# The layer norms of a ten-norm transformer stack: first moments of the last quarter taken earlier, last turned half evicted by ScalarE and VectorE together

## The reference, cut to what matters

```python
def layer_norm(h, g, b):
    mu = jnp.mean(hf, axis=-1, keepdims=True)
    var = jnp.mean(jnp.square(hf - mu), axis=-1, keepdims=True)
    y = (hf - mu) * lax.rsqrt(var + LN_EPS) * g + b
...
h = layer_norm(DEEPNORM_ALPHA * h + mix, ln1_g[l], ln1_b[l])
h = layer_norm(DEEPNORM_ALPHA * h + ffn, ln2_g[l], ln2_b[l])
```

## Time and profile before

| what | value |
|---|---|
| median of 3 runs | 3101.78 us (3094.33 to 3101.92) |
| the profiled execution's own time | 3095.23 us |
| its span, first to last instruction | 3093.4 us |
| TensorE busy | 2988.8 us, 97% |
| VectorE busy | 1920.4 us, 62% |
| ScalarE busy | 1347.9 us, 44% |
| GpSimd busy | 132.4 us, 4% |
| mean granted TensorE clock | 0.989 |

### The profile page before, as it was taken

The page is one execution under the profiler, slowest core; times in us unless marked ns, Lnnn a source line. Parts: engine busy times, 40 slices in busy tenths (PEclk is TensorE's granted clock), DMA queues, the critical chain, the costliest instruction groups (busy, mean ns, idle before and its releaser), DMA issues. The chain is left out here.

```text
span 3093.4 us, 53809 instructions
## 1 busy us (share of the span) xinstructions
PE 2988.8 (97%) x20906; PEld 2608.6 (84%) x20906; DVE 1920.4 (62%) x3659; ACT 1347.9 (44%) x2053; POOL 132.4 (4%) x62
## 2 busy tenths in 40 slices
PE   8998999999999999999999999999998999999898
PEld 7697889899898869888989989887777979777797
DVE  4489864787647648986478764755534564543546
ACT  4442444444444544244444444445424444442444
POOL 0061000000000006100000000000000000000000
PEclk9999999999999999999999999999999999999999
DMA  5243354544555424335454455553234545223444
GB/s 214 93 180 123 123 191 177 193 154 155 190 183 197 164 97 171 128 135 191 178 192 147 163 190 194 186 191 123 96 136 150 189 178 214 73 96 136 156 185 150
DMA packets 68022, 493.59 MB, mean 160 GB/s; under 512 B 7576, under 2 KB 7584, under 8 KB 8352
## 3 DMA queue, kind: packets, MB, share of 16 engines
q1 hardware_dynamic: 67568, 490.42, 43.6%
q0 software_dynamic: 304, 1.06, 0.1%
HBM read 490.39 MB, written 1.06 MB: 159 GB/s over the span
## 5 line engine op out<-in xcount | busy, mean ns | idle before, releaser
L780 DVE TENSOR_TENSOR ring_l<-ring,tile_h 128x1024 fp32r<-128x1024 f32 x648 | 765.0, 1222 | 667.9 <-ACT tile_h L735 663.8
L735 ACT ACTIVATE tile_h<-ring 128x1024 fp32r<-128x1024 f32 x644 | 645.7, 1051 | 533.2 <-PE ps L666 445.3
L634 PE MATMUL ps<-x_h,tile_h 128*128 128x256 f32 x2016 | 575.5, 285 | 2.1 <-issue 2.1
L635 PE MATMUL ps<-x_l,tile_h 128*128 128x256 f32 x2016 | 570.0, 283 | 0.0
L636 PE MATMUL ps<-x_h,ring_l 128*128 128x256 f32 x2016 | 569.9, 283 | 0.0
L634 PEld LDWEIGHTS ps<-x_h,tile_h 128*128 128x128 f32 x2016 | 386.4, 192 | 3.1 <-issue 2.8
L635 PEld LDWEIGHTS ps<-x_l,tile_h 128*128 128x128 f32 x2016 | 386.5, 192 | 0.2
L636 PEld LDWEIGHTS ps<-x_h,ring_l 128*128 128x128 f32 x2016 | 386.3, 192 | 0.0
L739 ACT ACTIVATE arena<-ps 128x512 f32 (+1 forms) x160 | 95.6, 597 | 432.2 <-PE ps L636 346.5
L664 PE MATMUL ps<-tile_h,w_even 128*128 128x512 f32 x640 | 249.5, 390 | 3.6 <-DVE w_even L805 3.6
L664 PE MATMUL ps<-tile_h,w_odd 128*128 128x512 f32 x640 | 249.3, 390 | 0.6 <-DVE w_odd L805 0.6
(11 more groups left out here) (322 smaller groups left out, 5598.8 us busy)
## 6 DMA issues: line engine op xcount, KB each, us to landing
ring<-stream SPq DMA_DIRECT2D x464, 1024.0 KB, 4.8
cs<-consts SPq DMA_DIRECT2D x1, 1712.5 KB, 8.6
x<-x_in SPq DMA_DIRECT2D x1, 1024.0 KB, 5.1
arena<-scratch POOLq DMA_DIRECT2D x1, 1024.0 KB, 7.8
out<-x SPq DMA_DIRECT2D x2, 512.0 KB, 2.7
tab<-table SPq DMA_DIRECT2D x1, 1.0 KB, 8.4
scratch<-arena POOLq DMA_DIRECT2D x1, 12.0 KB, 5.0
```

What stands on the lines that cost most here:

```text
L634: nc.tensor.matmul(out, uh[:, c, f], x_h[:, c, :], start=(c == 0), stop=False)
L635: nc.tensor.matmul(out, uh[:, c, f], x_l[:, c, :], start=False, stop=False)
L735: nc.scalar.activation(tile_h[:, j % 2, n], slot(k + j)[:, n], ACT.Copy).then_inc(hi_ready, 1)
L780: nc.vector.tensor_tensor(low_of(k + j)[:, n], slot(k + j)[:, n], tile_h[:, j % 2, n].bitcast(F32), ALU.subtract).then_inc(lo_ready, 1)
```

## The change

Two things are changed in each norm. First, VectorE takes the `bn_stats` of quarter (1,0) right after it has normalised tile 0, ahead of the wait for the last quarter; before, it was taken after the residual of the last quarter. Second, the eight turned chunks of token tile 1 are divided: ScalarE evicts chunks 0 to 3 (bank 6), and VectorE chunks 4 to 7 (bank 7), with its own semaphore `xt_dve`, between the last normalised half and the multiply by gamma. VectorE waits there until all transposes of the norm are done. All waits for the whole of `xT` now ask for both engines' counts (`turned`), and those of single chunks for the one that makes them (`chunk_turned`).

```diff
+        def turned(eng, m):
+            eng.wait_ge(xt_ready, 2 * KC + (KC + KC // 2) * m)
+            if m:
+                eng.wait_ge(xt_dve, KC // 2 * m)
...
+        def chunk_turned(eng, m, c):
+            if m == 0:
+                eng.wait_ge(xt_ready, KC + c + 1)
+            elif c < KC // 2:
+                eng.wait_ge(xt_ready, 2 * KC + (KC + KC // 2) * (m - 1) + (KC + c + 1))
+            else:
+                eng.wait_ge(xt_dve, KC // 2 * (m - 2) + (c + 1))
...
                     if fb == 0:
-                        pe.wait_ge(xt_ready, 2 * KC * m + (KC + c + 1))
+                        chunk_turned(pe, m, c)
...
             act_turned(act, n + 1, 0, 6, KC, which)
-            act_turned(act, n + 1, 1, 0, KC, which)
+            act_turned(act, n + 1, 1, 0, KC // 2, which)
...
             def moments(tt):
-                nc.vector.bn_stats(st[:, tt, 0, :], halves(tt, 0))
+                if tt == 0:
+                    nc.vector.bn_stats(st[:, tt, 0, :], halves(tt, 0))
                 step.after(nc.vector.bn_stats(st[:, tt, 1, :], halves(tt, 1)))
...
             residual(1, 0)
             normalize(0)
+            nc.vector.bn_stats(st[:, 1, 0, :], halves(1, 0))
             finished(dve, block, l, added)
             step.after(residual(1, 1))
             moments(1)
             normalize(1)
+            dve.wait_ge(xt_mm, 4 * n + 8)
+            for c in range(KC // 2, KC):
+                nc.vector.tensor_scalar(xT[:, c, P:2 * P], ps[7][:, (c - KC // 2) * P:(c - KC // 2 + 1) * P],
+                                        gb[:, which, 0, c:c + 1], gb[:, which, 1, c:c + 1],
+                                        ALU.mult, ALU.add).then_inc(xt_dve, 1)
             arrived(dve, block, l, k)
...
-            act.wait_ge(xt_ready, 4 * KC * l + 2 * KC)
+            turned(act, 2 * l)
             act_split_x(act)
...
-                pool.wait_ge(xt_ready, 6 * KC * l + (4 * LAYERS + 2) * KC)
+                turned(pool, 2 * LAYERS + 3 * l)
```

More of the change, by code:

```diff
@@ L211, in program @@
         acc_first, ln_half = sem("acc_first"), sem("ln_half")
-        xt_mm, xt_ready = sem("xt_mm"), sem("xt_ready")
+        xt_mm, xt_ready, xt_dve = sem("xt_mm"), sem("xt_ready"), sem("xt_dve")
         dve_step = sem("dve_step")
@@ L352, in carry_wait, with dve_norm @@
             nc.vector.memset(spare[:, cell:cell + 1], 0.0)
-        def dve_norm(dve, step, n, block, l, k, added):
+        def dve_norm(dve, step, n, block, l, k, added, which):
             def halves(tt, half):
@@ L1172, in scores_out @@
                                      ACT.Copy).then_inc(key_ev, 1)
-            act.wait_ge(xt_ready, 4 * KC * l + 4 * KC)
+            turned(act, 2 * l + 1)
             act_split_x(act)
@@ L1234, in dve_block1 @@
             nc.vector.tensor_copy(smA[:, 0:4], small[:, A_SUBG:A_SUBG + 4])
-            dve.wait_ge(xt_ready, 4 * KC * l + 2 * KC)
+            turned(dve, 2 * l)
             nc.vector.tensor_copy(gb[:, 0:2, :, :].rearrange("p n s c -> p (n s c)"), small[:, A_GB:A_GB + 4 * KC])
@@ L1299, in dve_block1 @@
                     sb_fail(pair + 2)
-            dve_norm(dve, step, l * 2, 1, l, A_LN1, A_WO + 3)
+            dve_norm(dve, step, l * 2, 1, l, A_LN1, A_WO + 3, 0)
             dve_split_x(dve, 2 * l + 1)
@@ L1443, in dve_block1 @@
             dve_down_block(dve, k + 7 * BLK, s + 6 * BLK, g + 3 * BLK, gate(2 * BLK))
-            dve_norm(dve, step, l * 2 + 1, 1, l, A_LN2, A_LN2 - 1)
+            dve_norm(dve, step, l * 2 + 1, 1, l, A_LN2, A_LN2 - 1, 1)
             step.close()
@@ L1763, in act_block2 @@
                      misc]
-            act.wait_ge(xt_ready, 6 * KC * l + (4 * LAYERS + 2) * KC)
+            turned(act, 2 * LAYERS + 3 * l)
             act.wait_ge(t_flip, 1)
@@ L1872, in act_block2 @@
             act_norm(act, norm + 1, 1)
-            act.wait_ge(xt_ready, 2 * KC * norm + 6 * KC)
+            turned(act, norm + 2)
             act_split_x(act)
@@ L2006, in dve_block2 @@
             norm = 2 * LAYERS + 3 * l
-            dve_norm(dve, step, norm, 2, l, B_LN1, B_MIX + 3)
+            dve_norm(dve, step, norm, 2, l, B_LN1, B_MIX + 3, 0)
             dve_units(dve, step, done_b + l * UNITS_B + len(mix_units), mem_units, plain_scale, banks=MEM_BANKS)
-            dve_norm(dve, step, norm + 1, 2, l, B_LN2, B_XO)
+            dve_norm(dve, step, norm + 1, 2, l, B_LN2, B_XO, 1)
             dve_split_x(dve, 2 * LAYERS + 2 * l + 1)
@@ L2018, in dve_block2 @@
             dve_down_block(dve, B_MLP + BLK, s + BLK, g, lambda h, i, j: h)
-            dve_norm(dve, step, norm + 2, 2, l, B_LN3, B_LN3 - 1)
+            dve_norm(dve, step, norm + 2, 2, l, B_LN3, B_LN3 - 1, 2)
             step.close()
```

## The result

| | before | after |
|---|---|---|
| median of the runs beside each other (4 and 4) | 3101.85 us | 3134.24 us (3128.42 to 3136.49) |
| ratio | | 1.0105 [1.0086, 1.0124] |
| the profiled execution, its span | 3095.23, 3093.4 us | 3136.49, 3134.7 us |
| mean granted clock | 0.989 | 0.979 |

The account below looks back on a forecast made before the run. TensorE, busy for 97% of the span, was taken as the bound. Terms 3.2 + 2.0 + 3.2 + 1.6 + 1.5 + 0.1 + 0.4 + 1.5 = 13.5 us took the median from 3101.78 to 3115.3 us, range 3103 to 3124.

Parts of the forecast that it names:

- The moments were worth 0: All ten norms: an earlier bn_stats gains 0; a rival at 0.06 had eight norms win 0.6 us each.
- The larger part of the mechanism: VectorE's queue behind the evictions (L393, L396, L817, L780) late by 1.5 or 2.0 us, less 0.3 to 0.4.
- 12 or more, and 2.7: Signs: TensorE's total wait for L780 at 12 us or more, from 4.7; ahead of L634 near 2.7, from 1.08.
- my 13.5: Sum over the norms, in us, added to the execution and the median; forecast of 11 to 17 us at 0.55.
- norm at 153: The load into the slot starts 1.5 us later, delaying ln_x and VectorE's ranking: 1.5 us.
- norm at 2016: Ahead of the second block's layers: late queue 1.5 us plus GpSimd's copy getting in between L393 and L396, 1.7: 3.2.
- norm at 2357: TensorE starts L634 when L780 is done: 2.0 less 0.4, 1.6 us, and the same in its twin at 2896.
- Four: about 0.83 us: VectorE's four evictions of 128 PSUM columns, in each norm: about 0.83 us until the next instruction can start.
- my upper bound of 1.1: VectorE's four evictions: 0.28 us each with no overlap, 1.1 us.
- the clock: Rival: three more falls of TensorE's clock lengthen waits behind L295; 13.5 + 4.8 = 18.3 us, 3120; chance 0.19.
- My argument against: Against more falls of TensorE's clock: the 2.82 us of idle time at 156 brought none.
- norm_read ... nothing but that meeting: Norms at 2311 and 2850: only ln_x meeting norm_read in L295 costs time, 0.2 us each, 0.4 in all.

Follow-up runs that it names:

- moments_only: Kernel before with only the bn_stats of quarter (1,0) moved early, ScalarE evicting all eight chunks: 3102.28 us, ratio 1.0010.
- delay_only: Kernel before, VectorE given the wait and four unused eviction-sized instructions (at 2016 the wait alone), ScalarE keeping all eight chunks: 3127.31 us, ratio 1.0090.
- after_again_1: Changed kernel, unaltered, traced a second time: 3130.06 us.
- before_again_1: Kernel before, unaltered, traced a second time: 3101.67 us.
- after_again_2: Changed kernel, unaltered, traced a third time: 3128.56 us.
- before_again_2: Kernel before, unaltered, traced a third time: 3101.17 us.
- after_late_waits_filled: Changed kernel with two thrown-away matmuls of 512 columns in TensorE's wait behind L295 (L309 after) in five norms: 3125.29 us, ratio 1.0074.
- evictions: Kernel before with only the second part, VectorE evicting chunks 4 to 7 of token tile 1: 3135.02 us, ratio 1.0118.
- root_after_four: Kernel before with the early moments and tile 1's root behind four of ScalarE's chunks in place of six: 3100.21 us, ratio 0.9991.
- before_filled: Kernel before with three thrown-away matmuls of 512 columns between the transposes of the two tiles in eight norms: 3102.79 us, ratio 1.0008.

## Why the prediction was wrong, by its own steps

**What held.** The bound was read rightly: what counts is what keeps TensorE idle or slow. The moments were worth 0, since the root is held by ScalarE's six chunks (`moments_only`). The larger part of the mechanism is the one forecast: L414, L417, L838 and L801 queued late behind the evictions. Idle time ahead of L838 is gone, the copy by GpSimd gets in, and the waits for `ring_l` and ahead of L655 rose from 4.7 to 9.6 and from 1.08 to 2.46 (forecast: 12 or more, and 2.7). `delay_only` shows it apart from everything else in the change. At full clock the loss is 12 to 13 us by the split above, against my 13.5. That nearness is partly luck: one term was 3 us too small, as shown next, so others were too large.

**The sum against the traces.** I compared the starts of the same TensorE instruction in two traces on both sides of each norm. Three pairs: the first traces, `after_again_1` less `before_again_1`, and `after_again_2` less `before_again_2`. In us:

```
                        forecast   first   second   third
norm at 153                1.5      2.6      0.5    -0.7
norm at 1016               2.0      3.7      2.4     0.5
norm at 1160               0.1      0.0      2.6    -0.2
norm at 2016               3.2      5.0      4.2     5.8
norm at 2311               0.2      0.8      0.8     0.8
norm at 2357               1.6      3.4      3.9     3.5
norm at 2546               1.6      0.5      2.4     1.6
norm at 2850               0.2      0.8      0.8     0.8
norm at 2896               1.6      1.1      3.9     1.6
the last                   1.5      2.8      1.6     1.9
all norms                 13.5     20.7     23.1    15.6
expert ranking and experts  -       1.1      3.7     6.6
first attention, layer 1    -      11.0      1.6     1.8
attention to the memory,
 layer 2                    -       7.2      0.0     4.8
start, second attention     -       1.1      0.0    -1.3
whole                     13.5     41.3     28.4    27.4
```

Single entries move by 2 to 3 us from pair to pair; either kernel's stretches at half clock come and go in them. Only the norms at 2016, 2311, 2357 and 2850 and the last lie above the forecast in all three.

**The step that failed first: "Four: about 0.83 us".** The term was mis-sized. L407's forty instructions take 0.403 us each, and the next instruction starts 1.28 us after the first of four: 0.32 us apart, not 0.20. I had priced them by L488, which reads PSUM with immediate factors. L407 takes its two factors from SBUF, one for each partition. In the same trace L488 (L509 there) takes 0.285 us for 128 columns and its neighbour L492 (L513), with one factor from SBUF, 0.346. That the factors make the difference is argued from these rows; no run separates it. So each norm's queue is 0.45 us later than I had it. That is more than my upper bound of 1.1, which came from the same row. In seven norms it is some 3 us: 13.5 becomes 16.6.

The Trainium skill, "VectorE: DVE Perf Modes", section on the TRN2 errata, puts the four at an estimated 1.03 us at one element a cycle, nearer than my 0.83. The trace's 1.28 lies above both. By the Trainium skill's figure my sum would have been larger by an estimated 1.4 us in seven norms, not by 1.6.

**The second, and the larger: "the clock" put among the rivals at 0.19, as a term of 0 in the sum.** It was what happened. By the mean clocks of all runs half-clock time grew from 87 to 127 us, some 20 us of added time, where the sum had 0 and the rival itself, three falls, 4.8: even its 3120 was 14 us short. In the norms half-clock time went from 20.5 to 34.1 us between the first traces, and from 22 to 33 in the mean of three traces of each: 11 us more of it is up to 6 us of added time, an estimate. `after_late_waits_filled` takes out 9 us by fills in the added waits. My argument against, that one wait of 2.82 us at 156 brought no fall, rested on one execution: the changed kernel's trace shows the fall at that same place behind the same wait (1.97 us for the transposes), the unchanged kernel has it there in `before_again_1`, and the earlier trace rows had shown one elsewhere. Waits that grow from about 1 to 2.5 us were exactly what the change brings. Sizes agree roughly: at 2357 1.6 + 0.45 leaves 1.4 to 1.9 us, at 2016 3.2 + 0.45 leaves 0.5 to 2.2, where one stretch of 3.4 us costs 1.7.

**The third: "norm_read ... nothing but that meeting".** With VectorE 2 to 4 us later, TensorE reaches `norm_read` before `ln_x` in norms where I had put no wait: 2.50 us in the norm at 2575 of two of three traces and 0.94 in the third, and 0.77 at 153 and 1160 in `after_again_2`. In the two norms with both roots first it is 0.54 each, where I had 0.2. In the first trace it waits 3.8 us for L417 in four norms. Part of it replaces the wait for `ring_l` further on, as at 2575, where that wait fell to 0.76 and the norm cost little.

**The rest.** The norms add 16 to 23 us in the three pairs, of 27 to 41. Against the medians' 32.4, some 9 to 17 us lie outside them. The 40 us more at half clock are some 20 us of time, and the other 12 to 13 us are delay at full clock. By the means of three traces of each kernel half-clock time grew by 11 us in the norms, by 10 in the first attention, by 11 in the attention to the memory and by 5 elsewhere. What of this growth beyond the norms is caused by the change is not settled. The attention to the memory falls to half clock in most traces of the changed kernel and in none of the three of before, but it does so now and then without evictions too, and filling it won 2.9 us at most; what decides it I can't show.

Expert ranking in the first layer has a loss of its own. TensorE's longest wait at L1040 there, at some 284 us, is either 7.4 to 8.0 or 12.2 us. It is 12.2 in all nine traces of kernels with VectorE late in every norm (changed, evictions, delay). Of the seven traces with one late norm at most and without fills it is 12.2 in two, `before` and `root_after_four`, and 7.4 to 8.0 in the other five, but it is 12.2 in all three with fills and no evictions. The ranking begins at 172.3 to 173.9 us in the three traces of the changed kernel and at 170.4 to 170.8 in those of the kernel before, 1.5 us or more later, as forecast. This may cost 4.2 us in place of the 1.5 of my sum, in the executions that were at 8. My first trace, at 12.2 already, could not show it; what tips the wait is open.

The range missed for one more reason. It was laid from a profiled execution 6.6 us below the median, of which I knew only the difference. Half-clock time differed by 21 and 26 us between it and two traces near the median.

## What to carry to other kernels

When work moves to an engine that is not the bound, price the wait in its queue too: the place (0.75 to 1.61 us of idle time, until all transposes were done) cost about as much as the four instructions (1.28 us), and one multiply put ahead of it gave back half of the loss, part of it as clock. An operation with factors from memory is priced by a row that has such factors too. Where a change lengthens waits of TensorE in front of dense matmuls, put the clock's cost into the sum and not among the rivals, and trace a kernel more than once before a single stretch is believed.

## What was unexpected in the hardware

- Executions of one kernel differ in where TensorE falls to half clock: 67.6, 94.0 and 88.2 us in three traces of the kernel before, with whole stretches of 20.5 us that are there or not. Its runs spread from 3091 to 3115 us, and the mean granted clock follows, from 0.990 to 0.980.
- The lower level was granted too where TensorE was mostly busy: busy for 53.72 of 57.00 us at a mean clock of 0.79.
- Filling a wait with thrown-away matmuls keeps the clock up (34.1 us to 0 in the norms) but gave between 0 and 9 us: by the mean clocks the fills of `before_filled` won 5 to 6 us and cost 8.
- Between two VectorE instructions that follow each other at once GpSimd's copy gets its turn: 1.73 us added to L417's pair (4.09 against 2.36), against a copy of 1.89 us.
